# Attention scores as two fp32r passes over stacked high and low rows, with the compressed branch spread over later steps

## What is computed

```python
s = jnp.einsum('bnqhgd,bnkhd->bnhgqk', qb, kb).astype(jnp.float32) * (dh ** -0.5)
...
p = jax.nn.softmax(s, axis=-1)
...
k_cmp = compress_blocks(rope(hd(kc, NSA_KV_HEADS), positions), cmp_k_pos, cmp_k_w1, cmp_k_w2)
v_cmp = compress_blocks(hd(vc, NSA_KV_HEADS), cmp_v_pos, cmp_v_w1, cmp_v_w2)
o_cmp, p_cmp = nsa_compressed_attention(q5, k_cmp, v_cmp)
...
o_b = (gates[..., 0:1] * o_cmp.reshape(B, T, NSA_HEADS, HEAD_DIM)
       + gates[..., 1:2] * o_sel.reshape(B, T, NSA_HEADS, HEAD_DIM)
       + gates[..., 2:3] * o_win)
mixed = jnp.concatenate([o_a.reshape(B, T, -1), o_b.reshape(B, T, -1)], axis=-1)
x = x + mixed @ w_out
```

## Time and profile before

| | |
|---|---|
| Time, median of 3 runs | 1576.52 us (1574.54 to 1577.93) |
| Time of the profiled execution | 1576.16 us |
| Its span, first to last instruction | 1574.3 us |
| PE busy | 1530.9 us, 97% of the span |
| DVE, ACT, POOL busy | 1228.3, 613.6, 493.5 us |
| Granted TensorE clock, mean | 0.996 of full speed |

### The profile page before, as it was taken

The page is one execution under the profiler, slowest core; times in us unless marked ns, Lnnn a source line. Parts: engine busy times, 40 slices in busy tenths (PEclk is TensorE's granted clock), DMA queues, the critical chain, the costliest instruction groups (busy, mean ns, idle before and its releaser), DMA issues.

```text
span 1574.3 us, 22581 instructions
## 1 busy us (share of the span) xinstructions
PE 1530.9 (97%) x8493; PEld 1352.7 (86%) x8493; DVE 1228.3 (78%) x2289; ACT 613.6 (39%) x1033; POOL 493.5 (31%) x323
## 2 busy tenths in 40 slices
PE   7998999999999989999999999999999999999997
PEld 5876887888889989999888887999999999999996
DVE  6637766347999999993766765889888889888986
ACT  6215554352221335663333333333333333333334
POOL 0000000215674830002111111555554555555520
PEclk9999999999999999999999999999999999999999
DMA  4510000423321547899998998999999999999971
GB/s 176 214 54 1 2 1 1 177 100 118 128 71 59 169 134 278 319 339 330 310 311 294 304 307 292 348 366 358 372 362 365 350 365 361 375 360 362 354 256 67
DMA packets 147164, 374.27 MB, mean 238 GB/s; under 512 B 11728, under 2 KB 76368, under 8 KB 144112
## 3 DMA queue, kind: packets, MB, share of 16 engines
q1 hardware_dynamic: 99488, 197.66, 36.3%
q0 software_dynamic: 37200, 138.56, 24.0%
q10 hardware_dynamic: 10368, 36.60, 6.2%
HBM read 334.11 MB, written 38.67 MB: 237 GB/s over the span
## 4 chain that ended last, share of the span: by engine, by line
PE 70%; DVE 25%; DMA 3%; issue 1%; ACT 1%; SPq 0%; ACTq 0%; DVEq 0%
PE bank L1651 30%; PE bank L1344 30%; PE bank L1429 3%; PE bank L1510 2%; DMA a_e<-act_dram 2%; DVE oh L1245 2%; DVE oh L1248 2%; DVE gp L1250 2%; DVE gp L1253 2%; DVE cand L1183 1%; DVE d_lo L1234 1%; PE bank L1494 1%; DVE key L1138 1%; DVE work L1158 1%; DVE ti L1157 1%
## 5 line engine op out<-in xcount | busy, mean ns | idle before, releaser
L1344 PE MATMUL bank<-h_hi,d_hi 128*128 128x384 f32 x1024 | 348.9, 341 | 2.8 <-DVE d_lo L1234 1.7
L1344 PE MATMUL bank<-h_lo,d_hi 128*128 128x384 f32 x1024 | 346.5, 338 | 0.0
L1344 PE MATMUL bank<-h_hi,d_lo 128*128 128x384 f32 x1024 | 346.2, 338 | 0.0
L1651 PE MATMUL bank<-u_hi,w_hi_e 128*128 128x512 f32 x768 | 301.3, 392 | 5.1 <-DVE u_lo L1229 5.1
L1651 PE MATMUL bank<-u_lo,w_hi_e 128*128 128x512 f32 x768 | 300.9, 392 | 0.0
L1651 PE MATMUL bank<-u_hi,w_lo_e 128*128 128x512 f32 x768 | 299.7, 390 | 0.0
L506 POOL DMA_INDIRECT p_in<-rows,p_row x128 | 160.0, 1250 | 412.5 <-DVE p_dot L1272 190.4
L506 POOL DMA_INDIRECT p_in<-up,p_row x128 | 170.8, 1334 | 199.0 <-DVE p_dot L1272 96.6
L1344 PEld LDWEIGHTS bank<-h_hi,d_hi 128*128 128x128 f32 x1024 | 192.7, 188 | 6.7 <-DVE d_lo L1234 2.7
L1344 PEld LDWEIGHTS bank<-h_lo,d_hi 128*128 128x128 f32 x1024 | 192.8, 188 | 3.2
L1344 PEld LDWEIGHTS bank<-h_hi,d_lo 128*128 128x128 f32 x1024 | 192.6, 188 | 0.0
(11 more groups left out here) (243 smaller groups left out, 2372.5 us busy)
## 6 DMA issues: line engine op xcount, KB each, us to landing
d_raw<-down SPq DMA_DIRECT2D x128, 512.0 KB
u_raw<-up SPq DMA_DIRECT2D x128, 512.0 KB
gates_dram<-ev ACTq DMA_DIRECT2D x12, 2048.0 KB, 6.7
g_e<-gates_dram SPq DMA_DIRECT2D x32, 768.0 KB
w_raw<-wts SPq DMA_DIRECT2D x9, 2048.0 KB, 7.9
act_dram<-f_act ACTq DMA_DIRECT2D x58, 192.0 KB
a_e<-act_dram SPq DMA_DIRECT2D x58, 192.0 KB
xt<-x_in SPq DMA_DIRECT2D x4, 512.0 KB, 8.8
```

The costliest lines, as they stand in the source:

```text
L1344: m = nc.tensor.matmul(out, a, b, start=(n == 0 and j == 0), stop=(n == last and j == 2))
L1651: m = nc.tensor.matmul(bank[2 * b + half][:], w[e % 3][:, tok], u[:, half * COLS:(half + 1) * COLS], start=(e == 0 and j == 0), stop=(e == ...
```

## The change

1. **Scores.** The fp32 matmul with zeros becomes two fp32r matmuls. The stationary tile `qp[g]` holds, for group g, the high parts of its queries in its own 64 rows and the low parts in the other 64; `k_hi[g]` holds the high parts of the keys of the group in both halves. One pass over 128 rows gives high by high plus low by high; a second over the group's 64 rows gives high by low, from `k_lo`. ACT makes `k_hi` (4 copies of 64x1536) and the high parts of the queries (4 of 64x2048), DVE the low parts (2 of 64x1536, 4 of 64x2048). The three memsets of POOL and the copy `q_g1` of ACT go.
2. **Compressed branch.** Keys and values at step 6, scores at steps 26 and 31, the DVE work at steps 10 to 13, 25 to 36 and 40 to 44, transpositions at 46, 52, 58 and 64 with the products two steps later and the additions four steps later. For blocks 0 and 1 the addition comes after SEL and WIN, through `o_tmp`. All of it uses bank 7.
3. **The rest.** `m_transposes` move to steps 70 to 85. Tile 4 is split in 8 pieces of 128x512 at steps 50 to 65. POOL loads `w1_v` later, to another place. Some semaphores are merged; the columns of `w_in` for the keys are permuted on the host.

```diff
-K_OF = {SWA: 0, SEL: 2, WIN: 3}
+K_OF = {SWA: 0, SEL: 1, WIN: 2}
+V_OF = {SWA: 0, SEL: 2, WIN: 3}
+K_CMP = 3
 STEP_QB = 3 * HEADS
-M_STEPS = (9, 12)
+C_AT = [46 + 6 * qb for qb in range(TB)]
+C_LATE = 2
+M_AT = {70 + 6 * b + 3 * half: (b, half) for b in range(TB - 1) for half in range(2)}
+W4_AT = {50 + 2 * k: k for k in range(KC)}
...
-            pool.wait_ge(S("w_hi_done"), 2)
-            pool.dma_start(w1_sb[1][:], w1[1].rearrange("p (l h) -> p l h", l=LP)).then_inc(S("w1v_loaded"), 16)
...
+            pool.wait_ge(S("pj_done"), 3 * TB)
+            pool.dma_start(w1_sb[1][:], w1[1].rearrange("p (l h) -> p l h", l=LP)).then_inc(S("w1v_loaded"), 16)
...
+                if u == 14:
+                    act.wait_ge(S("evT"), 12)
+                    for g in range(GROUPS):
+                        for to in range(2):
+                            nc.scalar.activation(k_hi[g][DH * to:DH * to + DH], kT[DH * g:DH * g + DH, 0:3], ACT.Copy)\
+                              .then_inc(S("k_hi"), 1)
...
+            def q_high(n):
+
+                for g in range(GROUPS):
+                    rows = slice(DH * g, DH * g + DH)
+                    nc.scalar.activation(qp[g][rows, n], qT[rows, n], ACT.Copy).then_inc(S("q_hi"), 1)
...
-            nc.scalar.activation(q_g1[DH:P], qT[DH:P], ACT.Copy).then_inc(S("q_moved"), 1)
-            split_w(4)
+            q_high(1)
...
+            def q_low(n):
+
+                for g in range(GROUPS):
+                    rows = slice(DH * g, DH * g + DH)
+                    other = slice(DH * (1 - g), DH * (1 - g) + DH)
+                    dve.wait_ge(S("q_hi"), 2 * n + g + 1)
+                    V.tensor_tensor(qp[g][other, n], qT[rows, n], f32(qp[g][rows, n]), ALU.subtract).then_inc(S("q_lo"), 1)
...
-                nc.tensor.matmul(bank[s % 3][:, 0:n], q_of[g][:, 0 if br == SWA else 1, j, qb * P:(qb + 1) * P],
-                                 kT[:, K_OF[br], k0:k0 + n], start=True, stop=False)
+                nc.tensor.matmul(bank[s % 3][:, 0:n], qp[g][:, which, j, tok], k_hi[g][:, K_OF[br], k0:k0 + n],
+                                 start=True, stop=False)
+                nc.tensor.matmul(bank[s % 3][:, 0:n], qp[g][own, which, j, tok], k_lo[own, K_OF[br], k0:k0 + n],
+                                 start=False, stop=False)
...
+                if s == 6:
+                    compress_out()
+                if s in (26, 31):
+                    compress_scores(s // 30)
...
-                    if s == 7:
+                    if s == 35:
...
-                    if s == 8:
+                    if s == 36:
                         V.tensor_tensor(cs, cs, over(c_max), ALU.subtract).then_inc(S("c_shift"), 1)
...
-                    if s == 13:
+                    if s == 44:
                         dve.wait_ge(S("c_p"), TB)
...
+                if s - 1 in W4_AT:
+                    k = W4_AT[s - 1]
+                    dve.wait_ge(S("w_piece_hi"), 4 + k + 1)
+                    V.tensor_tensor(w_lo[0][:, k], w_raw[0][:, k], f32(w_hi[0][:, k]), ALU.subtract).then_inc(S("w_piece_lo"), 1)
```

More of the change, by code:

```diff
@@ L192, in build @@
     wg_hi = sb("wg_hi", [P, KC, N_GATES], F32R)
-    w1_sb = [place("w1_k", [P, LP, CMP_HIDDEN], F32, after_w), sb("w1_v", [P, LP, CMP_HIDDEN])]
+    w1_sb = [place("w1_k", [P, LP, CMP_HIDDEN], F32, after_w), place("w1_v", [P, LP, CMP_HIDDEN], F32, base + 2 * 16384)]
+    at[0] += 4096
+    over_end = at[0]
+    k_hi = [sb(f"k_hi{g}", [P, 3, T], F32R) for g in range(GROUPS)]
     cx = [place(f"cx{i}", [P, LP, GROUPS, NC], F32, scratch + i * 4096) for i in range(2)]
@@ L545, in first_tile_high @@
                 nc.scalar.activation(w_hi[0][:, k], w_raw[0][:, k], ACT.Copy)\
-                  .then_inc(S("w0_hi_done" if part < 3 else "w_hi_done"), 1)
+                  .then_inc(S("w_piece_hi" if part < 3 else "w_hi_done"), 1)
             def second_tile_high(part):
@@ L552, in second_tile_high @@
                 nc.scalar.activation(w_hi[1][:, k], w_raw[1][:, k], ACT.Copy)\
-                  .then_inc(S("w_hi_done" if part else "w1_hi_done"), 1)
+                  .then_inc(S("w_hi_done" if part else "w_piece_hi"), 1)
             def x_high(b, half):
@@ L1009, in finish @@
                     V.tensor_tensor(out_a, o, co, ALU.mult).then_inc(S("o_free"), 1)
+                elif br == SEL and qb < C_LATE:
+                    V.tensor_tensor(out_b.rearrange("p (h d) -> p h d", h=HEADS), o, co, ALU.mult).then_inc(S("o_free"), 1)
                 else:
@@ L1418, in _ @@
                 t.then_inc(S("hid_ps"), 1)
-            q_of = (qT, q_g1)
             def query_keys(s):
@@ new lines, in compress_scores @@
+            def compress_scores(pair):
+                if pair == 0:
+                    pe.wait_ge(S("kc_done"), GROUPS)
+                    pe.wait_ge(S("vbd_done"), 8)
+                else:
+                    pe.wait_ge(S("c_masked"), 2)
+                for q in range(2 * pair, 2 * pair + 2):
+                    for j in range(HPG):
+                        c0 = (q % 2 * HPG + j) * GROUPS * CP
+                        m = nc.tensor.matmul(bank[7][:, c0:c0 + GROUPS * CP], qT[:, 1, j, q * P:(q + 1) * P],
+                                             kcT[:].rearrange("p g c -> p (g c)"), start=True, stop=True)
+                m.then_inc(S("c_s"), 1)
@@ L1550, in _ @@
                 if b == 0:
-                    pe.wait_ge(S("w_lo_done"), i + 1)
+                    if half == 0:
+                        pe.wait_ge(S("w_piece_lo"), 4 + KC)
+                    else:
+                        pe.wait_ge(S("w_lo_done"), 5)
                 if n >= 2:
```

239 lines of the change are left out of this document (124 added, 115 removed).

## The result

| | before | after |
|---|---|---|
| Median | 1575.83 us (4 runs, 1574.54 to 1577.93) | 1617.6 us (4 runs, 1615.69 to 1638.43) |
| Span of the profiled execution | 1574.3 us | 1616.7 us |
| Granted clock, mean | 0.996 | 0.961 |

The ratio of the times is 1.0297, with a 95% interval of 1.0266 to 1.0328: the change makes the kernel 3% slower. The prediction was 1,558 us, and even its slow rival ended at 1,587. The highest of the four times after the change (1638.43) is also the one with the lowest mean clock, 0.948, against 0.961 to 0.964 in the other three.

What follows compares the result with a forecast made beforehand. PE was taken to bound the mixer and most of the loop, block 0 waiting on PE and DVE in turn. Block terms -8.9 - 0.5 - 2.0 - 7.3 = -18.7 us from 1,576.2, with 0.3 back, gave 1,558 us; range 1,550 to 1,566.

Steps and rivals of the forecast that it cites:

- the price of a pass: Scores on PE: an fp32r pass taken at 0.12 us for 256 keys, 0.10 for 128; 17.9 us less PE work in all.
- Rival (c): Scores: fp32r at a quarter of its rate at 256 columns too, 0.44 us a pass; 1,587 us, slower; chance 0.04.
- Predicted 257.5: End of the attention loop: last scores, and with them the load of tile 5, near 257.5 us.
- Before the loop, 0 us: Ahead of the loop: ACT's and DVE's added splitting work hidden by L1409, 0 us; without that cover up to 5 us.
- The first transpose near 136.5: Block 0: PE's first transpose near 136.5 instead of 139.6 us, 3.1 us earlier, as the compressed branch's scores move to later steps.
- rival (d): Loop: loads mesh better, no lump costs, 1,552 us, or 1,551 if the table load runs ahead of the wait; chance 0.13.
- Block 0, -8.9 us: First block of the loop: ends near 154.1 instead of 163.0 us, with 2.5 us added for uneven PE and DVE work.
- Block 1, 28.8 us: Second block of the loop: PE 26.8 us plus 2.0 for two lumps of DVE work, 28.8 us, a change of -0.5.
- rival (a): Loop: DVE takes over, its lumps costing twice what was added, 1,564 us, or 1,566 if block 2 gains nothing; chance 0.18.
- Block 2, 36.1 us: Third block of the loop: PE 34.9 us plus 1.2 for DVE in the first eight steps, 36.1 us, a change of -2.0.
- Block 3, 38.5 us: Last block of the loop: PE 38.5 us instead of 45.8, DVE some 28, a change of -7.3.
- Behind the loop: After the last scores: same chain from tile 5 on, with a load of 8.69 us, moving as a whole.

Runs made afterwards that it cites:

- e1_full: Changed kernel with the second score pass over all 128 rows instead of 64: 1568.23 us, ratio to before 0.9955.
- e8_fill_72: Changed kernel, 64-row pass kept, with a 384-column bf16 filler matmul ahead of each unit's scores in blocks 0 to 2 only: 1580.89 us, ratio to before 1.0034.
- e6_full_fill: Changed kernel with all 128 rows in the second pass and 384-column bf16 fillers in blocks 0 and 1 only: 1561.0 us, ratio to before 0.9916.
- e5_swap: Changed kernel with the two score matmuls in the other order, the 64-row pass first: 1627.83 us (one run).
- e2_fp32: Changed kernel with its new order kept but the old scores, one fp32 matmul with zeros: 1572.62 us, ratio to before 0.9985.
- e7_full_fill_small: Changed kernel with all 128 rows in the second pass and 192-column bf16 fillers in blocks 0 and 1 only: 1559.64 us, ratio to before 0.9898.
- mended kernels: Changed kernel with 128 rows in the second pass and fillers in blocks 0 and 1, 384 or 192 columns: 1561.0 and 1559.64 us.

## Why the prediction was wrong

**The step that failed** is the price of a pass. "A pass at 256 costs no more than the 0.17 of 384", with a load of 0.10 as the floor at 128, rests on the earlier trace rows, and there every load has 128 rows. The second pass has 64. I had a sentence on it and drew nothing from it: that no row shows a 64-row load. The two passes of a unit were priced, with a fixed 0.07, at 0.27, 0.31, 0.41 and 0.53 us at 128, 256, 384 and 512 keys. Measured at full clock they take 0.52, 0.61, 0.72 and 0.83. With 128 rows in both (`e1_full`) they take 0.26, 0.32, 0.44 and 0.55, so fp32r itself was priced right within 0.03. Put into the sum of the prediction, the measured passes make the scores some 10 us more work for PE than before (24 x 0.24 + 40 x 0.12 + 16 x 0.02 - 16 x 0.08), instead of 17.9 less. Rival (c) came nearest, a pass too dear at 256 keys, but by the wrong mechanism, a rate of fp32r at narrow widths: the excess is as large at 512.

The trace of the kernel before had the sign, ahead of the loop, in loads of 24 and 62 rows that I had not read.

```profile
125.48 0.32 PEld L1403 LDWEIGHTS bank<-cst,gexp_T 24*128 24x128 f32 x4 [0.39 <-issue]
...
132.58 0.38 PE L1409 MATMUL bank<-w_v,cx 128*62 128x256 f32 x1
132.88 0.19 PEld L1416 LDWEIGHTS bank<-cst,hid_T 62*128 62x128 f32 x2 [0.39 <-issue]
132.89 0.33 PE L1416 MATMUL bank<-cst,hid_T 62*128 62x62 f32 x2
```

The 128-row matmuls of L1409 stand 0.22 us apart (7.12 us for 32), but the first 62-row one comes 0.31 behind the last of them, together with its load. The four 24-row loads, of 0.14 us each, lie within 0.32 us, so behind its like a load of few rows is not exposed. It seems to be the change of depth that costs, and not the small depth. No run isolates this (these are also transposes of another width), and none has two 64-row passes in a row.

**What it cost.** The exposure can be priced from two kernels whose clock is full. Block 3 has the same work in `e8_fill_72` and in `e6_full_fill` but for the depth of the second pass, and takes 44.8 and 38.7 us: 6.1 us, 0.25 a unit. Over the whole loop tile 5 starts at 283.96 and 263.13; less the 2.8 us for 24 fillers more in block 2, that is **18 us** of exposed loads.

The Trainium skill (TensorE: Matmul & The Clock Gate, LDWEIGHTS) says that the time of a load goes by its columns and not its rows. The records agree (0.18 us for 64 rows, 0.19 for 128); what I missed is that the same length can lie beneath a stream or behind it. The Trainium skill (TensorE: Matmul & The Clock Gate, The mechanism), on packing small matmuls, says that a load overlaps matmuls in flight only where its row group differs. The 64-row load behind 128 rows bears that out, its rows being in use; `e1_full` contradicts that sentence as put, since a load of the same 128 rows ran beneath their stream (the section also names a background weight buffer, whose use no record here shows). Between the score passes it held in all runs that the load behind a pass of the same depth is hidden and the one at a change of depth is not. It doesn't explain every spacing: in `e5_swap` the mask's matmul, 128 rows behind 128, still comes after 0.34 us, 0.10 more than in `e1_full`.

**The clock** is the second step that failed, and the larger loss. All prices in the prediction come from rows at a clock of 1.00, and that it would stay there was assumed without a word and had no rival. After to `e8_fill_72` tile 5 starts 39.3 us earlier; the 72 fillers in it cost up to 72 x 0.12 = 8.6 us more, so the fall cost some **40 to 48 us** (an estimate, since a filler beside a wait costs less). That the fall and not something else was the loss is shown by fillers that add work and gain 34 us in the changed kernel, and lose 7 us in the kernel before. Predicted 257.5, plus 18, plus 40 to 48, makes some 316 to 324; the trace has 323.24. (Both terms come from marks of the same traces, so the sum tests only the forecast of 257.5, and `e6_full_fill` with its fillers is 5.6 us behind that.)

What brings the fall about I can tell only so far: with fp32 scores (before; `e2_fp32` in the new order) the clock reads 1.00, or 0.92 in block 0; with two fp32r passes of 128 rows it has dips to 0.57; with a 64-row pass between exposed loads it stays at 0.50 for 87 us; with bf16 streams added it is back at 1.00. PE's recorded busy time doesn't tell them apart (16.19 of 23.40 us at clock 1.00 before, 87.00 of 87.00 at 0.50 after). The Trainium skill (TensorE: Matmul & The Clock Gate, HAM oscillation) puts such falls down to stretches in which PE is idle. For the first fall this trace doesn't agree: PE was busy 9.70 of the 10.00 us up to 136 us and all the time from there to 225, and in the kernel before PE had idle time in block 0 and kept its clock. The second fall does come behind a wait of 1.34 us; but the same product waits 1.5 us in `e2_fp32` and in `e7_full_fill_small`, where the clock reads 1.00, so the wait alone doesn't bring it about. The cause of the fall stays open. The fillers add streaming between the loads, but they are also of another type and change what lies around each load; and whether the exposed loads alone or the half-used rows too bring the clock down was not told apart.

**Point by point.**

- Before the loop, 0 us: right. Scores began at 133.51, with nothing late; without the cover of L1409 this would not have been free, and that wasn't tried.
- The first transpose near 136.5: 135.41, since the table load ran ahead of the wait, the small gain named in rival (d).
- Block 0, -8.9 us: 165.71 instead of 154.1 in the changed kernel. Where the passes are of full depth and the clock nearly full, 154.68 and 153.45: the working of the block was right.
- Block 1, 28.8 us: 59.1 in the changed kernel, at half clock. 32.4 in `e7_full_fill_small`, with PE at work for 28.97 (some 1.9 of them fillers, at their columns) and waiting for 3.4, not 2.0. For 2.1 of these it waits for ACT's exponentials, and ACT for DVE's maxima: 17.7 us for those of L1066 and 10.7 for those of L1063, in blocks 1 and 2 together. This is rival (a), a little of it, in a kernel in which it can be seen; in the changed kernel PE is busy for all of block 1 and DVE for less than half, so it had no part in the result.
- Block 2, 36.1 us: 53.7 after, 37.9 in both mended kernels.
- Block 3, 38.5 us: 44.8 after, 38.7 mended. The only block at full clock in both, and behind the forecast by the exposed loads.
- Behind the loop, "the chain moves as a whole": the load of tile 5 takes 8.03 us (8.69 before), and from its start to the end there are 1,293.5 us, against 1,298.1 before. Of these 4.6 us 0.7 are the load, and the rest lies where the change touches nothing; other kernels here have 1,294 to 1,298, and I have no cause for the difference.

The mended kernel's 1,559.6 lies by the forecast of 1,558, but this is partly luck: its loop ends 6.3 us later than forecast (0.6, 3.6, 1.8 and 0.2 us in blocks 0 to 3, of which the fillers are up to 1.9 in each of the first two), and its remainder is 2.3 us shorter than that of before. Nor is the gain made as forecast: the new order alone leaves the end of the loop where it was (`e2_fp32`), and all of it comes from the scores, with products of low parts and fillers that the changed kernel doesn't have.

## What to carry to other kernels

A matmul on fewer rows was no cheaper here, and next to matmuls of full depth it was dearer: 0.25 us a unit. Keep the depth of neighbouring matmuls the same, and let unused rows carry products that do no harm (zeros were not tried with fp32r). When PE's work is cut to shorter streams with loads between, ask whether the granted clock will hold, and look at it before anything else in the result: a busy share of 100% at a clock of 0.50 is not a bound but a symptom, and a few bf16 columns of no use can be cheaper than the fall. A row that carries the price of a new operation must have its shape in every respect, the rows of its stationary operand too.

## What was unexpected of the hardware

- A 64-row weight load behind a 128-row matmul, and a 128-row load behind a 64-row one, don't run beneath the stream: 0.26 us from one start to the next at 128 columns, against 0.13 with 128 rows in both.
- The granted clock fell to 0.50 with PE recorded busy 87.00 of 87.00 us, and read 1.00 with PE busy 16.19 of 23.40 (block 0 of the kernel before).
- 96 useless matmuls of 384 bf16 columns made the changed kernel 34 us faster and the kernel before 7 us slower.
- The table load of ACT started at 133.21, ahead of the wait for its operand (first exponential at 134.81), so that its 1.28 us were hidden.
